# Third layer's linear attention: head products among the next tile's level products, row products behind the sixth level

## The chip, the cores and the metric

The kernel runs on one core of a Trainium2 chip. The metric is the device time of one execution in microseconds (us). Several engines work side by side, each through its own list of instructions in order: TensorE (PE: matrix products, with PEld for the load of the stationary operand), VectorE (DVE), ScalarE (ACT), GpSimd (POOL), and SyncE (SP), which here only issues transfers from memory. They meet at semaphores.

## What is computed

The program runs two transformer blocks of two layers each, in 32-bit floats, on 512 latent tokens and 256 context tokens. The third layer (number 2 in the code) has a mixer that joins a Fourier mix and a gated linear attention. The part that matters, cut from the reference:

```python
def step(S, inp):
    qc, kc, vc, ac = inp
    b = jnp.cumsum(ac, axis=2)
    diff = b[:, :, :, None, :] - b[:, :, None, :, :]
    decay = jnp.exp(jnp.where(mask, diff, -jnp.inf))
    attn = jnp.einsum('bhid,bhjd,bhijd->bhij', qc, kc, decay)
    o = attn @ vc + jnp.einsum('bhid,bhde->bhie', qc * jnp.exp(b), S)
    ...
o_f, s_f = gla_scan(q, k, v, loga[0], s_f)
o_b, s_b = gla_scan(flip(q), flip(k), flip(v), flip(loga[1]), s_b)
o = o_f + flip(o_b)
o = o * lax.rsqrt(jnp.mean(o * o, axis=-1, keepdims=True) + EPS)
```

There are 4 heads with keys of 64 and values of 128. Besides this, each layer's modulation `silu(c) @ w_mod + b_mod` (1,024 by 6,144 per layer) has to be there before that layer starts; the fourth layer's is worked out during the third layer's attention.

## The kernel before

**Tiles and halves.** The 768 tokens are 6 tiles of 128 (`NT = 6`), and each tile has two halves, `dr = 0` and `dr = 1`: the scan forwards and the scan backwards. The loop counts them as `n = 2 * t + dr`, from 0 to 11. Tiles are counted from 0 here.

**Levels.** A decay between two rows of a tile is split by halving: 8 levels per half, in the order `LEVEL_ORDER = (7, 0, 1, 2, 3, 4, 5, 6)`. Level 7 is the diagonal; levels 0 to 6 are blocks of 64 rows down to 1. "Position i" below is the place in this order, 0 to 7. For each position TensorE multiplies the four heads' prepared queries and keys (line 1581) into one of two PSUM slots (`lv`, two slots in turns), and VectorE copies the wanted entries under a mask into the attention buffer `C_AT` (line 2397 at position 0, line 2399 at the others) and frees the slot. TensorE can be two positions ahead, not more.

**What feeds the levels.** VectorE forms exponents as differences of running sums (`differences`, line 2306), ScalarE takes absolute values and exponentials (`level_decays`, lines 3276 to 3282), GpSimd copies halves of queries and keys (`mixed_halves`, line 3589), VectorE multiplies the two (`coarse_products` line 2321, `next_products` line 2324, `products` line 2315). All this is done for later halves between the masks: in a first half after positions 5 and 6 there are two differences for the half after next, and ScalarE's `level_decays(n + 2, 0)` waits for the second of them. Behind the last mask of a second half come five differences in a row.

**Heads.** When both halves of a tile are masked (`L2_attention_ready`), TensorE multiplies `C_AT` with the values and the decayed queries with the carried state, all four heads in a row (line 1600), into PSUM banks 4 and 5 (`go`, one slot). ScalarE squares and sums each head and takes roots (lines 3311 and 3312), VectorE scales and gates (`heads_scaled` line 2374 and 2380, `heads_gated` line 2384) at positions 5 and 6 of the next tile's second half, and TensorE transposes the result (`turn`, line 1566). `C_AT` is one buffer for both halves of a tile, so VectorE waits with a new tile's masks until the heads before are done (`go.full`).

**Modulation.** Between the halves TensorE also does the fourth layer's modulation, twelve weight tiles of 2 MB: `mod_rows` (64 products, line 913) behind the eighth level of each half; ScalarE copies the row out (line 2924); `mod_columns` transposes it (line 922) behind position 2 of the next half; ScalarE copies that out (line 2930). `mod_rows` waits until ScalarE has taken the columns before, and `mod_columns` until it has taken the rows. The weight tiles come over SP's queue into a ring of two buffers; `mod_rows` frees one.

**TensorE's order around the change**, which is written out by hand: the 16 positions of a tile, `mod_rows` behind each 8, then `turn(t - 1)`, then the four heads of tile t, then the next tile. ScalarE's order in half n: `mod_columns` of n - 1; `level_decays`; the copy of `mod_rows`; and at the end of a second half the squares and roots of that tile's heads, which wait for `go.full`.

**Gates.** `GATE` holds two gates per token kind, spread over the partitions by GpSimd-issued transfers (`spread_gates`, line 3641): index 0 for the mixer's residual, index 1 for the feed-forward's.

Of the kernel before, what the change touches and what calls it, by code (L numbers as in the profile page):

```python
# [9 lines left out]
ACT = mybir.ActivationFunctionType  # L10
# [91 lines left out]
def build(nc, d, layers=(0, 1, 2, 3), debug=None):  # L102
# [3 lines left out]
    with ctxs:  # L106
# [360 lines left out]
        C_AT = GB[:, 1, :].rearrange("p (d h i) -> p d h i", d=2, h=4)  # L467
# [9 lines left out]
        def gla_orders():  # L477
            return ([4, 5, 0, 1, 2, 3], [5, 4, 3, 2, 1, 0])
# [396 lines left out]
        def _(pe):  # L875
# [601 lines left out]
            def mixer2():  # L1477
# [90 lines left out]

                for t in range(NT):
                    for dr in range(2):  # L1570
                        for v_ in LEVEL_ORDER:
# [13 lines left out]
                        if 2 in next_of:  # L1585
                            mod_rows(3, 2 * t + dr, 7)
                    if t:
                        turn(t - 1)
                    if t == 0:
                        pe.wait_ge(S("L2_states_ready"), 1)  # L1590
                    pe.wait_ge(S("L2_attention_ready"), 2 * t + 2)
                    b = 4 + place(go)
                    first = [o[0] for o in gla_orders()]
                    for h in range(GLA_H):
                        rows, a = slice((h % 2) * 64, (h % 2) * 64 + 64), h // 2
                        ops = [(C_AT[:, dr, h % 2 * 2 + a, :], C_V[:, t, h * 128:(h + 1) * 128]) for dr in range(2)]
                        ops += [(C_QB[rows, 2 * dr + a, t * 128:(t + 1) * 128], C_S[rows, dr * 6 + t, a * 128:(a + 1) * 128])
                                for dr in range(2) if t != first[dr]]
                        for j, (x, y) in enumerate(ops):
                            m = mm(bank(b + h % 2, 128, a * 128), x, y, start=j == 0, stop=j == len(ops) - 1)  # L1600
                    m.then_inc(go.full, 1)
# [388 lines left out]
        def _(dve):  # L1990
# [273 lines left out]
            def mixer2():  # L2264
# [122 lines left out]
                for n in range(2 * NT):  # L2387
                    t, dr = n // 2, n % 2
                    if t:
                        dve.wait_ge(go.full, t)  # L2390
                    for i, v_ in enumerate(LEVEL_ORDER):
                        ready(lv)
                        data = PS[:, i % 2 * 1024:i % 2 * 1024 + 1024].rearrange("p (s x) -> p s x", s=2)[:, :, 0:256]
                        at = C_AT[:, dr].rearrange("p (s a) i -> p s (a i)", s=2)
# [11 lines left out]
                        if dr == 0 and v_ in (4, 5) and n + 2 < 2 * NT:  # L2406
                            differences(n + 2, [v_ - 2])
                        if dr == 1 and v_ == 4 and t:
                            heads_scaled(t - 1)
# [291 lines left out]
            def paired_down(L, last_channels):  # L2701
# [32 lines left out]
                def added(q, tile, h):  # L2734

                    if (L, q, tile, h) == (0, 0, 0, 0):
                        dve.wait_ge(S("gates_in"), gates_so_far(0))
# [135 lines left out]
            for L in layers:  # L2873
# [4 lines left out]
                dve.wait_ge(S("gates_in"), gates_so_far(L) if L else 32)  # L2878
# [9 lines left out]
        def _(act):  # L2888
# [322 lines left out]
            def mixer2():  # L3211
# [76 lines left out]

                for n in range(2):
                    for part in range(2):  # L3290
                        level_decays(n, part)
                for n in range(2 * NT):
                    t, dr = n // 2, n % 2
                    if n and 2 in next_of:
                        mod_columns(3, n - 1, 7)
                    if dr == 1 and n + 1 < 2 * NT:
                        level_decays(n + 1, 1)
# [10 lines left out]
                    if dr == 1:  # L3308
                        act.wait_ge(go.full, t + 1)
                        for h in range(GLA_H):  # L3310
                            step(A(C_JUNK, bank(4 + h % 2, 128, h // 2 * 128), ACT.Square, accum_out=ST2[:, 32 + h:33 + h]))
                        step(A(ST2[:, 36:40], ST2[:, 32:36], ACT.Sqrt, scale=1.0 / GLA_DV, bias=EPSC))
                        post("head_rms_ready")
# [195 lines left out]
        def _(pool):  # L3509
# [137 lines left out]
            for n, L in enumerate(layers):  # L3647
# [16 lines left out]
                if L == 2:  # L3664
# [5 lines left out]
                    spread_gates(L)  # L3670
# [37 lines left out]
                else:  # L3708
                    pool.wait_ge(S("m_residual_ready"), tiles_before(L, "m") + 1)
                    bring("conv_vectors_in", CONV_ROWS[:, 0:384].rearrange("j (a p) -> j a p", a=3), d["w_ffn_conv_2"][l].rearrange("a (j p) -> j a p", p=128))  # L3710
                    bring("conv_vectors_in", CONV_ROWS[:, 384:512], rows(d["b_ffn_conv_2"][l]))
                if L >= 2:
                    sums_of_down_tokens(L, range(0, 2))
# [40 lines left out]
```

## Time and profile before

| | |
|---|---|
| median of 3 runs | 4030.51 us (4028.72 to 4032.4) |
| the profiled execution's own time | 4025.92 us |
| its span in the trace | 4024.1 us |
| TensorE busy | 3866.8 us, 96% |
| VectorE busy | 2207.2 us, 55% |
| ScalarE busy | 837.5 us, 21% |
| GpSimd busy | 599.3 us, 15% |
| level stage of the third layer, first level product to first output product | 2472.3 to 2621.6 us, 149.3 us |
| TensorE, VectorE, ScalarE busy in that stage | 123.4, 109.2, 77.8 us |

A busy share is a mean over stages with different limits. The span around the stage is 1.8 us shorter than the execution's time, and the profiled execution is 4.6 us below the median of the timed runs. In the timeline a row's start counts from the start of the span, "xN" is how many instructions are merged into the row, and a bracket at the end says how long the engine stood idle before the row and what released it. Matmuls overlap each other by some 0.1 to 0.2 us, so the distance between starts, and not the length, is what a group of products costs TensorE.

### The profile page before, as it was taken

To read this page: it belongs to the slowest core of one execution; us is meant where nothing else is said; L and a number is where in the kernel's file an instruction comes from. 1 tells how busy PE (TensorE), PEld (TensorE's weight loads), DVE (VectorE), ACT (ScalarE), POOL (GpSimd) and SP (SyncE) were. 2 spreads that over 40 slices of the span, in tenths; PEclk is the share of its full clock that TensorE was granted. 3 is DMA by queue.
4 is the path that set the end of the run, shared out by engine and by line. 5 is a ranking of instruction groups with operands and counts; after the bars stand their busy time and mean duration, and the time that the engine had idled before them with its cause. 6 is when DMAs were issued, how large, how long until landed. Compare 5 with 4: busy or idle time off the path is not lost.

```text
span 4024.1 us, 46147 instructions
## 1 busy us (share of the span) xinstructions
PE 3866.8 (96%) x17618; PEld 2307.7 (57%) x17618; DVE 2207.2 (55%) x3634; ACT 837.5 (21%) x1639; POOL 599.3 (15%) x944
## 2 busy tenths in 40 slices
PE   8999999999999999999999998899999999999998
PEld 5677455544455555458744645645555444758863
DVE  0354533366566556544556015737787765438876
ACT  1266111100122322211101114521100012531000
POOL 1000000133222431400132002200000430000023
PEclk9999999999999999999999998999999999999999
DMA  5355021355412222312344212411112452002234
GB/s 190 108 192 185 21 63 53 115 170 175 156 48 91 87 75 74 126 45 92 126 168 146 73 42 85 168 44 53 63 53 73 168 182 68 16 22 84 94 126 162
DMA packets 209784, 410.59 MB, mean 102 GB/s; under 512 B 5939, under 2 KB 92297, under 8 KB 209441
## 3 DMA queue, kind: packets, MB, share of 16 engines
q1 hardware_dynamic: 203712, 386.94, 28.4%
q0 software_dynamic: 5856, 20.73, 1.7%
q8 instruction: 141, 2.31, 0.2%
q14 instruction: 75, 0.61, 0.0%
HBM read 405.49 MB, written 2.16 MB: 101 GB/s over the span
## 4 chain that ended last, share of the span: by engine, by line
PE 88%; DVE 6%; ACT 3%; DMA 1%; issue 1%; POOL 1%; DVEq 0%; ACTq 0%; POOLq 0%; SPq 0%
PE PS L1210 28%; PE PS L1305 19%; PE PS L1170 5%; PE PS L1143 3%; PE PS L1784 3%; PE PS L1121 3%; PE PS L1798 3%; PE PS L913 2%; PE PS L1785 1%; PE PS L1945 1%; PE PS L1955 1%; PE PS L1429 1%; PE PS L1398 1%; PE PS L1123 1%; PE PS L1632 1%
## 5 line engine op out<-in xcount | busy, mean ns | idle before, releaser
L1210 PE MATMUL PS<-UT,RING 128*128 128x384 f32 (+1 forms) x2432 | 693.8, 433 | 10.8 <-ACT BIG L3011 9.7
L1210 PEld LDWEIGHTS PS<-UT,RING 128*128 128x128 f32 x2432 | 461.0, 190 | 205.5 <-issue 15.5
L1210 PE MATMUL PS<-BIG,RING 128*128 128x384 f32 (+1 forms) x1824 | 528.4, 433 | 0.8 <-DVE BIG L2846 0.5
L1210 PEld LDWEIGHTS PS<-BIG,RING 128*128 128x128 f32 x1824 | 346.0, 190 | 147.1 <-DVEq L2020 1.1
L1305 PE MATMUL PS<-RING,BIG 128*128 128x512 f32 x810 | 377.2, 593 | 2.8 <-POOL RES_TMP L3611 1.4
L3606 POOL TENSOR_TENSOR RES_TMP<-BIG 128x128 f32<-128x128 f32 x68 | 35.7, 525 | 1677.5 <-DVE BIG L2852 581.3
L2695 DVE TENSOR_TENSOR RING<-RING 128x512 f32<-128x512 f32 x135 | 107.0, 793 | 273.6 <-DMA RING<-ff_w_dram 161.5
L1305 PEld LDWEIGHTS PS<-RING,BIG 128*128 128x128 f32 x810 | 151.2, 190 | 183.2 <-issue 177.4
L1305 PE MATMUL PS<-RING,GATE 128*128 128x512 f32 x536 | 244.0, 596 | 6.1 <-DVE RING L2698 6.1
L1305 PE MATMUL PS<-RING,RES_TMP 128*128 128x512 f32 x544 | 245.3, 593 | 0.6 <-DVE RING L2698 0.6
L1305 PEld LDWEIGHTS PS<-RING,GATE 128*128 128x128 f32 x536 | 102.1, 191 | 136.6 <-issue 125.3
L1305 PEld LDWEIGHTS PS<-RING,RES_TMP 128*128 128x128 f32 x544 | 102.9, 190 | 131.9 <-issue 125.7
L3011 ACT ACTIVATE BIG<-PS 128x256 f32<-128x256 f32 (+1 forms) x62 | 26.3, 425 | 570.8 <-PE PS L1210 570.1
L1170 PE MATMUL PS<-RING,UT 128*128 128x512 f32 x320 | 139.2, 593 | 2.0 <-issue 1.2
L2110 DVE TENSOR_TENSOR RES_TMP<-PS,GATE 128x512 f32<-128x512 f32 x40 | 27.7, 692 | 206.5 <-PE PS L1170 137.1
L1784 PE MATMUL PS<-UT,RING 128*128 128x512 f32 x256 | 131.2, 594 | 2.3 <-DVE BIG L2490 1.0
L1121 PE MATMUL PS<-UT,RING 128*128 128x512 f32 x256 | 127.7, 594 | 1.0 <-ACT BIG L3222 1.0
L1798 PE MATMUL PS<-UT,RING 128*128 128x512 f32 x256 | 121.3, 599 | 0.0
L1143 PE MATMUL PS<-RING,UT 128*128 128x512 f32 x256 | 113.6, 606 | 2.5 <-ACT BIG L3340 0.9
L2555 DVE SCALAR_TENSOR_TENSOR BIG<-PS,BIG 128x510 f32<-128x510 f32 (+3 forms) x176 | 110.5, 628 | 6.3
L2696 DVE TENSOR_TENSOR RING<-RING 128x512 f32<-128x512 f32 x135 | 105.0, 778 | 0.0
L1170 PEld LDWEIGHTS PS<-RING,UT 128*128 128x128 f32 x320 | 60.0, 190 | 74.2 <-issue 73.2
(467 smaller groups left out, 5821.1 us busy)
## 6 DMA issues: line engine op xcount, KB each, us to landing
RING<-ff_w_dram SPq DMA_DIRECT2D x112, 1024.0 KB, 5.0
RING<-w_mod_dram SPq DMA_DIRECT2D x48, 2048.0 KB, 8.0
RING<-w_ffn_down_dram SPq DMA_DIRECT2D x55, 1024.0 KB, 5.0
RING<-w_ffn_up_dram SPq DMA_DIRECT2D x44, 1024.0 KB, 5.1
RING<-ssm_w_in_dram SPq DMA_DIRECT2D x8, 2048.0 KB, 7.8
RING<-ssm_w_out_dram SPq DMA_DIRECT2D x4, 2048.0 KB, 8.2
RING<-w_even_in_dram SPq DMA_DIRECT2D x4, 2048.0 KB, 8.3
GATE<-gates_dram POOLq DMA_DIRECT2D x12, 512.0 KB, 9.3
```

What stands on the lines that cost most here:

```text
L913: ins = mm(bank(bank_, 128)[32 * c:32 * c + 32, :], CVW[:, 4 * k + lc:4 * k + lc + 32], w[:, k, c * 128:(c + 1) * 128], start=k == 0, stop ...
L1121: m = mm(PS[:, x:x + LAT], a, UT[:, k, 0:LAT], start=k == 0, stop=k == KD - 1)
L1123: m = mm(PS[:, x + 512:x + 512 + nctx], a, UT[:, k, LAT:LAT + nctx], start=k == 0, stop=k == KD - 1)
L1143: m = mm(bank(first_bank + t, cols[1] - cols[0]), inp[:, kk, t * 128:(t + 1) * 128], w[:, k, cols[0]:cols[1]], start=kk == 0, stop=kk == k ...
L1170: m = mm(bank(t), inp[:, kk, t * 128:(t + 1) * 128], w[:, k, :], start=kk == 0, stop=kk == kn - 1)
L1210: m = mm(bank(bank_, n), a[:, k, :], b[:, k, :], start=k == 0, stop=k == 3)
L1305: return mm(bank(banks[name]), a, b, start=s == 0, stop=last)
L1784: mm(PS[:, x:x + LAT], a, UT[:, k, 0:LAT], start=k == 0, stop=k == KD - 1)
L1798: m = mm(bank(4 + q), wz[:, k, q * 128:(q + 1) * 128], UT[:, k, 0:LAT], start=k == 0, stop=k == KD - 1)
L2555: ins = V.scalar_tensor_tensor(y[:, lo:hi], PS[:, x + lo + o:x + hi + o], w(k), y[:, lo:hi], ALU.mult, ALU.add)
L2695: step.go(V.tensor_tensor(t3, b22, b12, ALU.subtract))
L2696: step(V.tensor_tensor(t1, b12, b11, ALU.subtract))
```

## The change

Six things change, all in the third layer.

1. The attention buffer becomes two, used in turns by tile: the old one and `GATE[:, 1, 0, :]`, which VectorE clears once, in half 0 behind position 5. VectorE's wait on the heads moves back by one tile.
2. The heads of tile t - 1 move into the first half of tile t: one head behind each of positions 1, 2, 3 and 4 (behind `mod_columns` where position 2 has both). The last tile's heads stay behind its levels.
3. `mod_rows` moves from behind position 7 to behind position 5, in every half.
4. `turn(t - 1)` stays behind the tile's levels, and now nothing of line 1600 follows it except in the last tile.
5. ScalarE's squares and roots move from the end of half 2t + 1 to half 2t + 2, behind the copy of `mod_columns`.
6. The second gate is brought after the first residual tile instead of at the start of the layer, and waits are counted accordingly.

```diff
-        C_AT = GB[:, 1, :].rearrange("p (d h i) -> p d h i", d=2, h=4)
+        C_AT = tuple(x.rearrange("p (d h i) -> p d h i", d=2, h=4) for x in (GB[:, 1, :], GATE[:, 1, 0, :]))
...
+                def head(t, h):
+                    if h == 0:
+                        if t == 0:
+                            pe.wait_ge(S("L2_states_ready"), 1)
+                        pe.wait_ge(S("L2_attention_ready"), 2 * t + 2)
+                        go_bank[t] = 4 + place(go)
+                    b = go_bank[t]
+                    rows, a = slice((h % 2) * 64, (h % 2) * 64 + 64), h // 2
+                    ops = [(C_AT[t % 2][:, dr, h % 2 * 2 + a, :], C_V[:, t, h * 128:(h + 1) * 128]) for dr in range(2)]
+                    ops += [(C_QB[rows, 2 * dr + a, t * 128:(t + 1) * 128], C_S[rows, dr * 6 + t, a * 128:(a + 1) * 128])
+                            for dr in range(2) if t != first[dr]]
+                    for j, (x, y) in enumerate(ops):
+                        m = mm(bank(b + h % 2, 128, a * 128), x, y, start=j == 0, stop=j == len(ops) - 1)
+                    if h == GLA_H - 1:
+                        m.then_inc(go.full, 1)
...
-                        for v_ in LEVEL_ORDER:
+                        for i, v_ in enumerate(LEVEL_ORDER):
...
                             if v_ == 1 and 2 in next_of and t + dr:
                                 mod_columns(3, 2 * t + dr - 1, 7, MOD_ROWS[2])
-                        if 2 in next_of:
-                            mod_rows(3, 2 * t + dr, 7)
+                            if t and dr == 0 and 1 <= i <= GLA_H:
+                                head(t - 1, i - 1)
+                            if i == 5 and 2 in next_of:
+                                mod_rows(3, 2 * t + dr, 7)
                     if t:
                         turn(t - 1)
-                    if t == 0:
-                        pe.wait_ge(S("L2_states_ready"), 1)
-                    pe.wait_ge(S("L2_attention_ready"), 2 * t + 2)
...
+                for h in range(GLA_H):
+                    head(NT - 1, h)
...
-                    if t:
-                        dve.wait_ge(go.full, t)
+                    if t >= 2:
+                        dve.wait_ge(go.full, t - 1)
...
-                        at = C_AT[:, dr].rearrange("p (s a) i -> p s (a i)", s=2)
+                        at = C_AT[t % 2][:, dr].rearrange("p (s a) i -> p s (a i)", s=2)
...
+                        if n == 0 and v_ == 4:
+                            step(V.memset(GATE[:, 1, 0, :], 0.0))
...
-                    if (L, q, tile, h) == (0, 0, 0, 0):
-                        dve.wait_ge(S("gates_in"), gates_so_far(0))
+                    if L in (0, 2) and (q, tile, h) == (0, 0, 0):
+                        dve.wait_ge(S("gates_in"), gates_so_far(L))
...
-                dve.wait_ge(S("gates_in"), gates_so_far(L) if L else 32)
+                dve.wait_ge(S("gates_in"), gates_so_far(L) - (32 if L in (0, 2) else 0))
...
+                def head_roots(t):
+                    act.wait_ge(go.full, t + 1)
+                    for h in range(GLA_H):
+                        step(A(C_JUNK, bank(4 + h % 2, 128, h // 2 * 128), ACT.Square, accum_out=ST2[:, 32 + h:33 + h]))
+                    step(A(ST2[:, 36:40], ST2[:, 32:36], ACT.Sqrt, scale=1.0 / GLA_DV, bias=EPSC))
+                    post("head_rms_ready")
...
                     if n and 2 in next_of:
                         mod_columns(3, n - 1, 7)
+                    if dr == 0 and t:
+                        head_roots(t - 1)
                     if dr == 1 and n + 1 < 2 * NT:
                         level_decays(n + 1, 1)
...
-                    if dr == 1:
-                        act.wait_ge(go.full, t + 1)
...
+                head_roots(NT - 1)
...
-                    spread_gates(L)
+                    spread_gates(L, (0,))
...
+                    if L == 2:
+                        spread_gates(L, (1,))
```

## Rows read from the trace of the kernel before

**Rows 1.** Page, part 4: shares of the chain that ended last

```profile
PE 88%; DVE 6%; ACT 3%; DMA 1%; issue 1%; POOL 1%; DVEq 0%; ACTq 0%; POOLq 0%; SPq 0%
```

**Rows 2.** Stretches: span, busy PE, PEld, DVE, ACT, POOL, clock, DMA share, GB/s

```profile
2523.31:2532.76 9.45, 7.52 (x132) 6.03 (x131) 7.65 (x14) 7.65 (x22) 2.43 (x9) 1.00 0.12 37
...
2532.76:2548.67 15.91, 12.50 (x164) 10.24 (x165) 11.77 (x22) 8.01 (x16) 5.82 (x20) 1.00 0.71 244
...
2564.40:2569.90 5.50, 5.42 (x84) 4.51 (x81) 4.82 (x8) 0.28 (x1) 2.38 (x10) 0.61 0.03 9
```

**Rows 3.** Stretch, line 1600 alone, tile 1: span, busy PE, PEld, clock, DMA share, GB/s

```profile
2517.56:2522.68 5.12, 5.12 (x32) 4.15 (x32) 1.00 0.90 303
```

**Rows 4.** Timeline, VectorE ahead of tiles 2, 1, 4, 5: start, us, engine, line, idle

```profile
2518.77 2.53 DVE L2306 TENSOR_TENSOR UT<-BIG 128x256 f32<-128x256 f32 x5
...
2523.31 0.73 DVE L2397 COPY_PREDICATED GB<-UT,PS 128x512 f32<-128x512 uint8 x1 [2.00 <-PE PS L1581]
...
2497.80 0.73 DVE L2397 COPY_PREDICATED GB<-UT,PS 128x512 f32<-128x512 uint8 x1 [2.86 <-PE PS L1581]
...
2575.37 0.73 DVE L2397 COPY_PREDICATED GB<-UT,PS 128x512 f32<-128x512 uint8 x1 [3.35 <-PE PS L1581]
...
2599.83 0.73 DVE L2397 COPY_PREDICATED GB<-UT,PS 128x512 f32<-128x512 uint8 x1 [1.12 <-PE PS L1581]
```

**Rows 5.** Timeline, first half of tile 2, TensorE and VectorE

```profile
2524.09 0.71 PE L1581 MATMUL PS<-UT 64*128 64x128 f32 x8 [0.45 <-DVE GB L2397]
...
2524.74 0.33 PE L922 MATMUL PS<-CS,RES_TMP 128*128 128x128 f32 x1
...
2524.92 0.45 DVE L2399 COPY_PREDICATED GB<-UT,PS 128x256 f32<-128x256 uint8 x1 [0.40 <-PE PS L1581]
...
2524.99 1.16 PE L1581 MATMUL PS<-UT 64*128 64x128 f32 x16
...
2529.25 0.73 DVE L2399 COPY_PREDICATED GB<-UT,PS 128x256 f32<-128x256 uint8 x1
...
2529.44 1.95 PE L913 MATMUL PS<-RING,CVW 128*32 128x128 f32 x64
...
2531.32 0.71 PE L1581 MATMUL PS<-BIG 64*128 64x128 f32 x8
```

**Rows 6.** Timeline, tile 2, ScalarE and what follows from it

```profile
2525.79 0.28 ACT L3311 ACTIVATE UT<-PS 128x128 f32<-128x128 f32 x1
...
2527.38 1.28 ACT L3312 ACT_TABLE_LOAD   x1
...
2528.67 0.30 ACT L3312 ACTIVATE ST<-ST 128x4 f32<-128x4 f32 x1
...
2530.55 1.65 ACT L3276 ACTIVATE UT<-BIG 128x128 f32<-128x128 f32 x6 [1.29 <-DVEq L2020]
...
2536.57 0.44 DVE L2399 COPY_PREDICATED GB<-UT,PS 128x256 f32<-128x256 uint8 x1 [0.99 <-PE PS L1581]
```

**Rows 7.** Timeline, second half of tile 2

```profile
2537.15 0.72 PE L1581 MATMUL PS<-UT 64*128 64x128 f32 x8 [0.19 <-DVE GB L2399]
...
2540.47 0.75 DVE L2399 COPY_PREDICATED GB<-UT,PS 128x256 f32<-128x256 uint8 x1
```

**Rows 8.** Line 2296, the other clearing of a 1,024-column buffer: ns min/median/max

```profile
L2296 DVE MEMSET GB<- x1: 912/912/912, 2439.6 to 2439.6; 128x1024 f32 x1
```

**Rows 9.** Timeline, first half of the last tile and the step behind it

```profile
2604.85 2.03 DVE L2399 COPY_PREDICATED GB<-UT,PS 128x256 f32<-128x256 uint8 x3
...
2609.44 0.73 DVE L2397 COPY_PREDICATED GB<-UT,PS 128x512 f32<-128x512 uint8 x1 [1.39 <-PE PS L1581]
```

**Rows 10.** Timeline, row product in tile 3 at the low clock

```profile
2566.07 3.23 PE L913 MATMUL PS<-RING,CVW 128*32 128x128 f32 x64
```

**Rows 11.** Buffer GATE from 2440 to 3300 us: first product with the second gate

```profile
L2741 DVE TENSOR_TENSOR GATE<-GATE x6: 691/826/828, 3185.0 to 3264.2; 128x512 f32<-128x512 f32 x6
```

**Rows 12.** Page, part 6: KB each, us to landing

```profile
RING<-w_mod_dram SPq DMA_DIRECT2D x48, 2048.0 KB, 8.0
```

More of the change, by code:

```diff
@@ L1567, in turn @@
                     m.then_inc(gt.full, 1)
+                first = [o[0] for o in gla_orders()]
+                go_bank = {}
+                def head(t, h):
[13 more added lines that the diff above has]
+                        m.then_inc(go.full, 1)
                 for t in range(NT):
                     for dr in range(2):
-                        for v_ in LEVEL_ORDER:
+                        for i, v_ in enumerate(LEVEL_ORDER):
                             if v_ in (0, 4):
@@ L1584, in mixer2 @@
                                 mod_columns(3, 2 * t + dr - 1, 7, MOD_ROWS[2])
-                        if 2 in next_of:
-                            mod_rows(3, 2 * t + dr, 7)
+                            if t and dr == 0 and 1 <= i <= GLA_H:
+                                head(t - 1, i - 1)
+                            if i == 5 and 2 in next_of:
+                                mod_rows(3, 2 * t + dr, 7)
                     if t:
                         turn(t - 1)
-                    if t == 0:
-                        pe.wait_ge(S("L2_states_ready"), 1)
-                    pe.wait_ge(S("L2_attention_ready"), 2 * t + 2)
[L1592 to L1601, printed above, removed]
+                for h in range(GLA_H):
+                    head(NT - 1, h)
                 if 2 in next_of:
@@ L3307, in mixer2 @@
                         level_decays(n + 2, 1)
-                    if dr == 1:
-                        act.wait_ge(go.full, t + 1)
[L3310 to L3313, printed above, removed]
+                head_roots(NT - 1)
                 if 2 in next_of:
```

## The prediction

> **What bounds the kernel now.** I read the page's chain of waits first [rows 1]: TensorE holds most of it, but that is the mean of a long program, and the change touches one stage of 149 us. So I went to the busy time by stretch of one ordinary tile there, tile 2 [rows 2]. Its first half takes 9.45 us and its second 15.91. In the first half TensorE and VectorE are busy 7.52 and 7.65 us, in the second 12.50 and 11.77: two engines that hand work to each other, neither full. What counts is who waits where, and that is in the timeline.
>
> Between two tiles VectorE waits. Its five differences end at 2518.77 + 2.53 = 2521.30, and its first mask of tile 2 starts only at 2523.31, after 2.00 us of idling on TensorE [rows 4]. TensorE was then behind with the row product and the four heads, 5.12 us for 32 instructions, which is 1.28 us a head [rows 3]. The same wait is 2.86 us ahead of tile 1, 3.35 ahead of tile 4 and 1.12 ahead of tile 5 [rows 4]; ahead of tile 3 it is as in tile 2. Inside the first half it is VectorE that paces: TensorE's 64 products of line 913 run from 2529.44 to 2531.32, and VectorE needs what follows them only at the end of the half [rows 2, 5]. In that half the row product costs nothing today.
>
> **The change, part by part.**
>
> **The wait between tiles goes.** With the heads moved, TensorE has only the transposes and positions 0 and 1 to do there (0.65 us a position [rows 5], from 2524.09 to 2524.74), while VectorE is busy 2.53 us with the differences alone. The second attention buffer lets the first mask start. So the mask comes when the differences end: 2.00 us earlier in each of tiles 2 and 3. Ahead of tile 4 I also take 2.00 and not 3.35, since the 1.35 between them stands behind a row product that took 3.23 us instead of 1.95 at a low clock [rows 5, 10], which the change doesn't remove. Ahead of tile 5 it is 1.12. Late next is VectorE itself.
>
> **The heads and the row product lengthen the first half.** TensorE works in order, so everything put among the positions pushes the later ones. The first head is free: it is issued during the differences, before VectorE begins the tile. From there I add up TensorE's path in tile 2 from the start of position 2 at 2524.09, which waits for the first mask as now [rows 5]: position 2, 0.65; columns, 0.25 (2524.74 to 2524.99); three heads, 3 x 1.28 = 3.84; positions 3, 4 and 5, 3 x 0.65 = 1.95; row product, 1.88 (2529.44 to 2531.32). That is 8.57 us, so position 6 starts at 2532.66. A mask starts 0.83 us after its products (2524.09 to 2524.92), so that of position 6 starts at 2533.49. Today it starts at 2529.25. **The delay is 4.24 us.** VectorE can't make it up: in this stretch it has only masks and products that each wait for the position before.
>
> The delay passes on whole. The second difference behind that mask is what ScalarE waits for at 2530.55, after idling 1.29 us [rows 6]; the exponentials that follow release the row's copy, the columns, position 3 of the second half and, at 2536.57 after 0.99 us of idling, VectorE. That chain moves by the same 4.24, and so does VectorE's own.
>
> **The squares and roots** move with the heads. ScalarE is waiting for the last head with the level decays and the copy of the rows queued behind it, and TensorE's columns wait for that copy. The last head ends 0.65 + 0.25 + 3.84 + 2 x 0.65 = 6.04 us after 2524.09, at 2530.13. The squares take 1.59 (2525.79 to 2527.38), the table load and the root 1.59 more (to 2528.67 + 0.30) [rows 6], so they end at 2533.31. The exponents come 1.30 us behind the mask of position 6 (2529.25 to 2530.55), at 2534.79. The cover is 1.5 us and this costs nothing; without it each microsecond would go straight into the second half.
>
> **The row product of a second half** is hidden there. Position 5 starts at 2537.15 [rows 7]; with 0.65 + 1.88 + 0.83 the mask of position 6 can start at 2540.51, against 2540.47 now, because VectorE scales the heads in between. Cost 0.04, taken as nothing. Then the transposes: they still wait for the gating, and positions 0 and 1 behind them have the time of the differences.
>
> **Tile 0** has no heads in its first half. It gets the clearing of the second buffer, and the nearest row is the same instruction on another buffer of 1,024 columns, 0.91 us [rows 8]. Its second half has no scaling to hide the row product, which costs between 0 and 1.88 us. Against these stands the wait of 2.86. The sum lies between -1.95 and -0.07; I take the middle, -1.0.
>
> **The last tile.** The heads that move into its first half are those of tile 4, where one direction starts and a head has 6 instructions instead of 8: an estimate of 0.96 us each from [rows 3]. The path becomes 7.61 us, and the mask of position 6 starts 0.78 + 7.61 + 0.83 = 9.22 us after the first mask. Today it is the second of the three masks that begin at 2604.85 [rows 9], some 0.48 later, which is 5.50 us after the first at 2599.83. Delay 3.72; less 1.39, the wait ahead of the second half [rows 9], which stood for a row product that comes earlier now. Its second half has a thinner VectorE and nothing for the half after next, so the row product costs 0 to 1.88 us; I take 0.95. Together +3.3. The last heads stay where they were.
>
> **Costed at nothing**: the second gate is fetched behind the first residual tile, and its first use is at 3185.0 [rows 11], over 500 us later; GpSimd has only the two issues more there and two fewer at the layer's start. SP's queue: the row products free its weight buffers a few us earlier or later, a load takes 8.0 us [rows 12], and a buffer is wanted again a tile later, some 25 us [rows 2]; if that cover went, one load would show. VectorE's new wait on the heads of two tiles ago is long past.
>
> **Sum**: tile 0 -1.0; tiles 1, 2 and 3, 3 x (4.24 - 2.00) = +6.7; tile 4, 4.24 - 1.12 = +3.1; tile 5 +3.3. Together +12.1 us. Against the profiled execution's own 4025.92 us that is 4038.0; the median of the runs shown lies 4.6 us above that execution, so the forecast on its scale is 4042.6 us, 0.30% slower. A measurement of this kernel can tell about 0.2%, 8 us, from no change.
>
> **The rivals.**
>
> **Faster.** The heads fall into TensorE's gaps and only the waits between tiles change: 2.86 + 2 x 2.00 + 3.35 + 1.12 = 11.3 us, which gives 4019. For it: TensorE idles 1.93 + 3.41 us in a tile [rows 2], more than the heads that VectorE waits for. Against it: the point at which it decides is the room in the first half, 1.93 us, and three heads with the row product bring 5.72. It needs the heads to overlap the positions, and in the rows nothing on TensorE does.
>
> **Within 0.2%.** The row product of a first half stays hidden, as in the second: 5 x 1.88 = 9.4 us fewer, 4033. It decides by VectorE's work behind position 5, one mask and one difference, 0.9 us, against 1.88. Against it is also that each of these masks waits for TensorE in the sum, so VectorE has nothing in store.
>
> **The clock.** TensorE's granted clock was 0.61 of full speed on average from 2564.40 to 2569.90 [rows 2], a time partly at 1.2 instead of 2.4 GHz, and a row product took 3.23 us there instead of 1.95 [rows 5, 10], 1.66 times as long. Ahead of it TensorE had the thin start of a second half; the same start in tile 2 went by at 1.00 [rows 2]. The change makes first halves dense, and the starts of second halves no denser. A first half that falls into the low clock lengthens by up to 0.66 x 8.57 = 5.7 us; two of them give 4054. Now these products are on VectorE's path, so a fall costs more than today. The Trainium skill, TensorE: Matmul & The Clock Gate, section "HAM oscillation", says that gaps between groups of matmuls drop the clock again and that work without gaps keeps it up. By that rule the first halves would hold the clock and the risk would lie with the second halves; no run here shows that yet.
>
> **How the numbers follow.** The forecast has 0.62, with a range of its own of 4037 to 4049 us: the two halved bounds give 1.9 us, the clock of one half 5.7. The clock rival has 0.13, within 0.2% 0.13, faster 0.12. The range from 4030 to 4056 takes in the small rival and most of the clock's; left out are the faster case and a tail, 0.17. Slower by over 0.2% lies above 4038.6: 0.55 of the forecast's share and the clock's 0.13, 0.68. Same: 0.20. Faster: 0.12.
>
> **What would show it.** In the changed profile VectorE's 2 us wait ahead of each tile is gone; in first halves of tiles 1 to 4 the mask of position 6 starts 10.2 us after the first mask instead of 5.9; new waits of VectorE on line 1581 stand ahead of the masks of positions 3, 4, 5 and 6; a tile takes 27.6 us instead of 25.4. It is wrong if a first half stays near 9.5 us, if ScalarE ends the roots after the exponents, or if the row product of a second half shows.

## The result and the profile after

The changed kernel takes 4068.72 us (4067.85 to 4073.6) against 4029.61 for the kernel before on the same chip: 1.0096 times as long, 95% interval 1.0084 to 1.0108. The sign is as forecast, the size three times as large: 39 us, not 12, and outside the range.

Head and part 1 of the page of the changed kernel:

```profile
span 4066.8 us, 46148 instructions
...
PE 3894.7 (96%) x17618; PEld 2332.0 (57%) x17618; DVE 2206.4 (54%) x3635; ACT 837.4 (21%) x1639; POOL 596.8 (15%) x944
```

VectorE, ScalarE and GpSimd are as busy as before; TensorE runs the same 17,618 products and is busy 28 us longer. So it is the same work, done slower or waited for.

A half runs from VectorE's first mask of that half to its first mask of the next (line 2397, now 2407). In us, with the granted clock as a share of full speed:

| | first half, tiles 1 / 2 / 3 / 4 / 5 | second half, tiles 0 / 1 / 2 / 3 / 4 |
|---|---|---|
| before | 9.45 / 9.45 / 9.46 / 9.45 / 9.61 | 14.31 / 16.06 / 15.91 / 17.24 / 15.01 |
| after | 17.39 / 17.48 / 15.88 / 17.42 / 16.28 | 13.20 / 16.53 / 16.54 / 15.71 / 16.20 |
| clock before | 1.00 / 1.00 / 1.00 / 1.00 / 1.00 | 1.00 / 0.89 / 1.00 / 0.80 / 1.00 |
| clock after | 0.71 / 0.71 / 0.79 / 0.71 / 0.69 | 0.87 / 0.79 / 0.79 / 0.78 / 0.79 |

First halves are 37.0 us longer in sum, second halves 0.4 shorter; tile 0's first half adds 0.9 (10.74 for 9.84) and the last tile's second half with its heads 3.8 (15.97 for 12.17, up to the first output product). That is the whole 41.4 us of the stage; some 2 us more stand behind it, in output products that still run at the low clock. The rows of tile 2, to set beside [rows 2] (stretch, busy PE, PEld, DVE, ACT, POOL, clock, DMA share, GB/s):

```profile
2530.51:2547.99 17.48, 15.07 (x153) 12.79 (x153) 7.57 (x14) 9.27 (x25) 2.05 (x9) 0.71 0.18 52
...
2547.99:2564.53 16.54, 11.43 (x141) 9.52 (x141) 11.73 (x23) 6.38 (x14) 5.79 (x20) 0.79 0.57 202
```

VectorE works as long as before in either half. The timeline of the same tile:

```profile
2527.36 0.71 PE L1584 MATMUL PS<-BIG,GATE 128*128 128x128 f32 x4
...
2527.77 2.52 DVE L2316 TENSOR_TENSOR UT<-BIG 128x256 f32<-128x256 f32 x5
...
2530.51 0.73 DVE L2407 COPY_PREDICATED GB<-UT,PS 128x512 f32<-128x512 uint8 x1 [0.22 <-DVE UT L2316]
...
2531.29 0.71 PE L1600 MATMUL PS<-UT 64*128 64x128 f32 x8 [2.58 <-DVE GB L2407]
...
2537.61 1.22 PE L1584 MATMUL PS<-BIG,GATE 128*128 128x128 f32 x4
...
2540.76 3.08 PE L913 MATMUL PS<-RING,CVW 128*32 128x128 f32 x64
...
2542.89 0.30 ACT L3305 ACTIVATE ST<-ST 128x4 f32<-128x4 f32 x1
...
2544.53 0.72 DVE L2409 COPY_PREDICATED GB<-UT,PS 128x256 f32<-128x256 uint8 x1 [2.77 <-PE PS L1600]
...
2545.80 1.65 ACT L3288 ACTIVATE UT<-BIG 128x128 f32<-128x128 f32 x6 [2.62 <-DVEq L2030]
```

The wait ahead of the tile is gone, as forecast: the mask at 2530.51 follows the differences and no longer TensorE [rows 4]. In its place TensorE has idled 2.58 us when it starts position 2 at 2531.29. Soon after that everything it does takes longer: four instructions of a head 1.22 us, where those of the first head took 0.71 at 2527.36, and the row product 3.08 instead of 1.95 [rows 5]. The mask of position 6 starts at 2544.53, which is 14.0 us after the first mask; the forecast had 10.2, and it was 5.9 before. The clock in finer stretches of that tile:

```profile
2528.60:2531.29 2.69, 0.10 (x1) 0.00 (x1) 2.29 (x6) 2.38 (x8) 1.41 (x4) 1.00 0.82 308
...
2531.29:2532.80 1.51, 1.51 (x15) 1.27 (x17) 0.88 (x2) 1.39 (x2) 0.00 (x0) 1.00 0.00 0
...
2533.00:2543.00 10.00, 10.00 (x88) 8.71 (x88) 3.11 (x6) 4.60 (x13) 1.94 (x8) 0.50 0.01 2
...
2543.70:2545.30 1.60, 1.23 (x24) 0.97 (x16) 0.74 (x2) 0.00 (x0) 0.00 (x0) 1.00 0.21 22
...
2545.30:2550.79 5.49, 2.15 (x24) 1.60 (x25) 4.80 (x9) 4.78 (x10) 1.69 (x6) 0.92 0.99 350
...
2550.79:2555.00 4.21, 4.21 (x41) 3.66 (x45) 2.29 (x6) 1.86 (x3) 0.06 (x1) 0.50 0.12 41
```

TensorE idles (0.10 us of work in 2.69), goes on at full speed for some 1.6 us, and then stands at the lower of its two levels, 1.2 GHz, for some ten us, though it never stops working in them. Then full speed again; a thin start of the second half (2.15 us of work in 5.49); then the lower level once more. The first halves of tiles 1, 4 and 5 look like this too; in tile 3 the clock came back earlier (15.88 us at 0.79).

### The profile page after: what moved, and what is told of

It reads as the page before. It is cut to its first block, busy times and chain, and to the rows that moved or that the text cites. A ratio compares the mean times of both kernels' runs of the same rounds, so it can differ in the third digit from the quotient of the medians.

```text
span 4066.8 us, 46148 instructions
## 1 busy us (share of the span) xinstructions
PE 3894.7 (96%) x17618; PEld 2332.0 (57%) x17618; DVE 2206.4 (54%) x3635; ACT 837.4 (21%) x1639; POOL 596.8 (15%) x944
## 4 chain that ended last, share of the span: by engine, by line
PE 89%; DVE 5%; ACT 3%; issue 1%; DMA 1%; POOL 0%; DVEq 0%; ACTq 0%; SPq 0%; POOLq 0%
PE PS L1210 27%; PE PS L1305 19%; PE PS L1170 5%; PE PS L1143 3%; PE PS L1794 3%; PE PS L1121 3%; PE PS L1808 3%; PE PS L913 2%; PE PS L1795 1%; PE PS L1955 1%; PE PS L1965 1%; PE PS L1429 1%; PE PS L1398 1%; PE PS L1600 1%; PE PS L1123 1%
## 5 line engine op out<-in xcount | busy, mean ns | idle before, releaser
L913 PE MATMUL PS<-RING,CVW 128*32 128x128 f32 x3072 | 104.0, 293 | 0.4 <-DMA RING<-w_mod_dram 0.4
```

The lines of the kernel that those rows point to most:

```text
L913: ins = mm(bank(bank_, 128)[32 * c:32 * c + 32, :], CVW[:, 4 * k + lc:4 * k + lc + 32], w[:, k, c * 128:(c + 1) * 128], start=k == 0, stop ...
```

## The experiments

Theory A: the forecast's count is right at full speed, and what it lacked is the clock, which falls because the change leaves TensorE idle ahead of position 2 (and thinly used at the start of a second half). Rivals: B, the mix of head and level products is slow by itself; C, the row product in the middle of the half does the harm and the clock is secondary. For each run the table has the ratio to the kernel before with its interval, and means over tiles 1 to 4.

| run | median us | ratio | first half, clock | second half, clock |
|---|---|---|---|---|
| before | 4029 to 4030 | | 9.45, 1.00 | 16.06, 0.92 |
| after | 4068.72 | 1.0096 (1.0084 to 1.0108) | 17.04, 0.73 | 16.25, 0.79 |
| e1 | 4046.19 | 1.0041 (1.0027 to 1.0055) | 12.75, 1.00 | 16.28, 0.79 |
| e2 | 4040.57 | 1.0027 (1.0016 to 1.0037) | 12.55, 0.89 | 15.31, 0.83 |
| e3 | 4058.80 | 1.0070 (1.0053 to 1.0087) | 13.17, 0.91 | 16.90, 0.90 |
| e4 | 4028.04 | 0.9997 (0.9987 to 1.0006) | 9.45, 1.00 | 16.12, 0.90 |
| e5 | 4025.09 | 0.9985 (0.9976 to 0.9994) | 10.66, 1.00 | 14.74, 0.80 |
| e6 | 4039.65 | 1.0024 (1.0015 to 1.0033) | 12.75, 1.00 | 14.21, 1.00 |
| e7 | 4043.82 | 1.0034 (1.0021 to 1.0048) | 9.84, 1.00 | 17.52, 0.81 |
| e8 | 4021.16 | 0.9978 (0.9969 to 0.9987) | 11.76, 0.84 | 13.39, 0.93 |
| e9 | 4025.91 | 0.9989 (0.9980 to 0.9999) | 9.67, 1.00 | 14.81, 0.97 |
| e10 | 4057.88 | 1.0079 (1.0063 to 1.0095) | 16.11, 0.78 | 14.19, 1.00 |
| e11 | 4023.36 | 0.9985 (0.9976 to 0.9994) | 9.66, 0.98 | 13.96, 0.98 |

### e1: the idle place ahead of position 2 filled

```diff
                                 head(t - 1, i - 1)
+                                if i == 1:
+                                    for _ in range(7):
+                                        mm(bank(4, 128, 256), ident, ident, start=True, stop=True)
```

> The changed kernel with seven extra 128x128 products behind each first head (tiles 1 to 5), into a corner of PSUM that nothing reads; 14 instructions at 0.16 us, about 2.2 us, in the place where TensorE idles 2.6 us between its first head and position 2. Theory A (that idling lets TensorE's clock fall, and the fall is what the forecast lacked): first halves of tiles 1 to 3 go from 17.4 to about 13.7 us at a granted clock near 1.0 instead of 0.71, the program takes 4037 to 4049 us. Theory B (the low clock comes from the thin second halves or from the mix of head and level products itself): first halves stay at 17 us and 0.7, the program stays at 4065 to 4072 us.

Stretches of tile 2, and TensorE's timeline in it:

```profile
2527.65:2540.42 12.77, 10.37 (x153) 8.78 (x153) 7.59 (x13) 9.27 (x24) 2.25 (x9) 1.00 0.24 72
...
2540.42:2556.13 15.71, 12.84 (x155) 10.89 (x155) 11.86 (x22) 6.39 (x14) 5.83 (x20) 0.78 0.58 210
```

```profile
2528.43 0.72 PE L1600 MATMUL PS<-UT 64*128 64x128 f32 x8 [0.84 <-DVE GB L2410]
...
2529.78 0.37 PE L1584 MATMUL PS<-BIG 64*128 64x128 f32 x1
...
2529.80 0.37 PE L1600 MATMUL PS<-UT 64*128 64x128 f32 x1
...
2534.32 1.96 PE L913 MATMUL PS<-RING,CVW 128*32 128x128 f32 x64
...
2541.20 1.22 PE L1600 MATMUL PS<-UT 64*128 64x128 f32 x8 [1.32 <-DVE GB L2410]
...
2546.66 2.32 PE L913 MATMUL PS<-RING,CVW 128*32 128x128 f32 x64
```

Adding work made the program 23 us faster than the changed kernel. First halves run at full speed in all five tiles and take 12.77 us instead of 17.48 in tile 2. B is out: the mix of products is not slow by itself. It is even cheaper than counted. Rows of line 1584 (heads) and line 1600 (levels) stand 0.02 us apart at 2529.78 and 2529.80: products of 64 rows from either overlap. From position 2 to the row product it is 2534.32 - 2528.43 = 5.89 us, where the forecast's terms make 6.69. The second halves are as slow as in the changed kernel: position 2 starts at 2541.20 after 1.32 us of idling and takes 1.22 us, and the row product 2.32.

### e10 and e6: the other two corners

The same with three such products behind position 1 of a second half and three behind position 2, in the slots of `lv` that TensorE holds then; e10 has these alone, e6 has them and those of e1.

```diff
-                            b = place(lv) * 2
+                            if not (t and dr and i == 3):
+                                b = place(lv) * 2
...
+                            if t and dr and i == 1:
+                                for _ in range(3):
+                                    m = mm(bank(b, 128, 256), ident, ident, start=True, stop=True)
                             m.then_inc(lv.full, 1)
+                            if t and dr and i == 2:
+                                b = place(lv) * 2
+                                for _ in range(3):
+                                    mm(bank(b, 128, 256), ident, ident, start=True, stop=True)
```

> The changed kernel with the idle products in the second halves alone, the idling ahead of position 2 left open. With e1 (first place filled alone) and e6 (both) this makes the four corners. If each place sets the clock of what follows it: first halves stay near 17.4 us at 0.71, second halves go to about 14.2, the program to 4052 to 4060 us. If the second place also feeds the next first half, first halves drop too and the program comes under 4048 us.

> The kernel of e1 with six more idle products in each second half of tiles 1 to 5: three behind position 1, three ahead of the columns behind position 2, where TensorE idles 1.3 us twice; nothing reads them. Theory A2 (the second halves run long because the clock falls behind that thin start, and the row product behind position 5 then stands on VectorE's path): clock near 1.0 in both halves, second halves 14.0 us instead of 15.7 to 16.9, first halves 12.8 as in e1, the program at 4032 to 4038 us. If the second halves' length has another cause: clock near 1.0 but 15.7 to 16.9 us, the program at 4043 to 4050 us.

Stretches of e10: first and second half of tile 1, first half of tile 2; then TensorE's position 2 in the first half of tile 3:

```profile
2495.82:2513.17 17.35, 15.48 (x157) 13.26 (x158) 7.56 (x13) 8.70 (x23) 1.98 (x9) 0.70 0.22 70
...
2513.17:2527.41 14.24, 10.19 (x151) 8.22 (x149) 11.85 (x22) 6.45 (x15) 5.89 (x20) 1.00 0.66 238
...
2527.41:2541.72 14.31, 12.44 (x158) 10.72 (x159) 7.58 (x13) 9.28 (x24) 2.25 (x9) 0.88 0.20 64
...
2556.68 1.23 PE L1601 MATMUL PS<-UT 64*128 64x128 f32 x8 [2.58 <-DVE GATE L2415]
```

Stretches of e6, first and second half of tile 2:

```profile
2522.27:2535.04 12.77, 10.90 (x158) 9.38 (x159) 7.58 (x13) 9.27 (x24) 2.24 (x9) 1.00 0.24 74
...
2535.04:2549.23 14.19, 11.88 (x164) 9.79 (x163) 11.78 (x22) 6.40 (x14) 5.83 (x20) 1.00 0.66 236
```

The corners come apart cleanly. Where a place is filled the half behind it runs at 0.99 to 1.00, in every tile from 1 to 5 for the first place and from 1 to 4 for the second; where it isn't, it doesn't, whatever the other place does. In e10 the open place gave 17.35 us in tile 1 but 14.31 in tile 2: the same idling, of 2.6 us, is paid for with different lengths of low clock. In tile 3 the clock was low before TensorE went back to work: position 2 itself took 1.23 us. e6 is the forecast's own kernel at full speed: halves of 12.8 and 14.2 us, where the forecast's terms give 13.7 and 13.9. Its median is 10 us above before, 1.7 above what was expected. That makes the 39 us, as an estimate, some 10 of order and some 29 of clock; what the idle products themselves cost is not told apart. (The executions of e6 spread from 4033.4 to 4044.0 us, those of the kernel before beside them from 4025.4 to 4036.1.)

### e2: only the heads moved

The changed kernel with `if i == 7` instead of `if i == 5` ahead of `mod_rows`.

> The changed kernel with the modulation's row product back behind position 7 in every half. Theory A: the idling ahead of position 2 is still there, so the first halves still run at about 0.7, shorter only by the row product of about 3 us at the low clock: 14 us each, the program at 4048 to 4060 us. Theory C (the row product in the middle of a first half is what makes it long; the clock is secondary): first halves near 11.8 us at a clock near 1.0, the program at 4030 to 4036 us.

TensorE's rows at position 2 of tiles 1, 2, 4 and 5, and the first halves of tiles 1, 2 and 4:

```profile
2501.50 0.71 PE L1600 MATMUL PS<-UT 64*128 64x128 f32 x8 [1.40 <-DVE GATE L2407]
...
2528.18 1.01 PE L1600 MATMUL PS<-UT 64*128 64x128 f32 x8 [1.88 <-DVE GB L2407]
...
2582.40 0.71 PE L1600 MATMUL PS<-UT 64*128 64x128 f32 x8 [2.55 <-DVE GB L2407]
...
2612.96 0.71 PE L1600 MATMUL PS<-UT 64*128 64x128 f32 x8 [2.77 <-DVE GATE L2407]
```

```profile
2500.72:2511.75 11.03, 10.10 (x153) 8.67 (x153) 7.53 (x13) 7.91 (x22) 2.16 (x9) 1.00 0.42 161
...
2527.39:2540.06 12.67, 11.65 (x153) 10.01 (x153) 7.55 (x13) 8.54 (x23) 2.24 (x9) 0.87 0.28 105
...
2581.61:2597.01 15.40, 14.53 (x153) 12.78 (x153) 7.50 (x13) 8.91 (x24) 2.04 (x9) 0.67 0.18 70
```

Neither expectation fits. The row product behind position 7 now uses up part of the idle place, differently in each tile, and that makes the run worth having: after 1.40 us of idling the half runs at 1.00 and takes 11.03 us, after 1.88 at 0.87 and 12.67, after 2.55 at 0.67 and 15.40. In these tiles, and in tile 3 (0.37 us of idling, 11.11 us at 1.00), the first half's length goes with the idling ahead of it. Tile 5 does not fit: it had the longest idling, 2.77 us, and ran at 0.85, for 11.50 us. C is out: in tile 4 the row product isn't there, and the half is still slow; in e1 it is there, and the half takes 12.77 us at full speed.

### e3 and e7: only the row product moved

In the kernel before, with the heads where they were:

```diff
-                        if 2 in next_of:
-                            mod_rows(3, 2 * t + dr, 7)
+                            if i == 5 and 2 in next_of:
+                                mod_rows(3, 2 * t + dr, 7)
```

> The kernel before with only the row product moved behind position 5 in every half; the heads stay behind each tile. By the forecast's way of counting the second halves of tiles 1 to 3 lose 1.9 us each of VectorE's wait and the first halves gain 0.5 (position 5 is early there without heads), tile 4 loses 0.6, tile 0 about 1: the program 4 to 7 us faster than before, 4023 to 4026 us, at a clock near 1.0 throughout. If the row product in a first half is as costly as in the changed kernel, the program is level with the kernel before or slower, 4029 to 4036 us.

TensorE's row product in the first half of tile 2:

```profile
2539.45 3.28 PE L913 MATMUL PS<-RING,CVW 128*32 128x128 f32 x64 [2.20 <-ACT MODC L2930]
```

This was not the test that was meant. `mod_rows` waits for ScalarE's copy of the columns before, and in the old order that copy stands behind the squares and roots: 2.20 us of waiting. The program is slower than either expectation. The clock goes with this wait too, though no head stands among the positions: in tile 1 TensorE waited 1.54 us and the first half stayed at 1.00, in tiles 2 to 5 it waited 2.19 to 3.07 us and they ran at 0.88. e7 puts ScalarE in the changed kernel's order as well:

```diff
...
                         mod_columns(3, n - 1, 7)
+                    if dr == 0 and t:
+                        head_roots(t - 1)
...
-                    if dr == 1:
-                        act.wait_ge(go.full, t + 1)
...
+                head_roots(NT - 1)
```

> The kernel of e3 (row product behind position 5, heads where they were) with ScalarE's squares and roots behind the copy of the columns, as in the changed kernel. In e3 TensorE waited 2.2 to 3.1 us ahead of each first half's row product for that copy. Without this wait the first halves come to 10 us instead of 13.7, the second to 16 to 17 if the low clock stays, the program to 4035 to 4043 us; 4029 to 4033 us if the clock holds. If that wait was not the cause, it stays at 4055 us or more.

Halves of tile 2, and in its second half VectorE's mask of position 6 and the transposes:

```profile
2530.60:2540.44 9.84, 7.53 (x133) 6.06 (x131) 7.70 (x13) 7.64 (x21) 2.24 (x9) 1.00 0.28 85
...
2540.44:2558.21 17.77, 14.74 (x164) 12.38 (x165) 11.84 (x22) 8.03 (x16) 5.82 (x20) 0.81 0.55 193
```

```profile
2550.03 0.72 DVE L2399 COPY_PREDICATED GB<-UT,PS 128x256 f32<-128x256 uint8 x1 [1.23 <-PE PS L1581]
...
2551.59 0.66 PE L1566 MATMUL PS<-CS,GB 128*128 128x128 f32 x4 [1.23 <-DVEq L2020]
```

First halves go to 9.84 us: in them the row product costs 0.4, close to the forecast's count for a half without heads (0.5 in e3's text). The second halves are 1.5 us longer than before, and the program 14 us. Before, the row product stood behind position 7, where TensorE waits for the gating anyway, and filled it. Now that place is 1.23 us of idling, and the row product stands ahead of position 6, in a half at 0.81 of the clock, so VectorE waits 1.23 us for that position. Why the clock is lower in these halves than before, 0.81 for 0.92, no run shows. The forecast had this move at nothing.

### e8: idling without the change

The kernel before with `ops = ops[:1]` for each head: one product is done, the others are left out.

> The kernel before with one of the four products of each head (of the three in tiles 4 and 5) done and the others left out: the backward half of the attention and the carried state are missing from the heads. TensorE is short of 3.8 us of work between tiles and idles there instead, and VectorE's wait of 2.0 us ahead of a tile goes. If idling there by itself drops the clock (theory A without the head products among the levels), first halves run at 0.7 to 0.9 and take 10 to 11 us instead of 9.45. If the fall needs the products that follow, the clock stays at 1.0 in first halves, they take 9.4 us, and the program is 7 to 11 us faster than before, 4018 to 4022 us.

TensorE in the first halves of tiles 2, 3 and 5, and the stretch of tile 5's:

```profile
2519.21 0.72 PE L1581 MATMUL PS<-UT 64*128 64x128 f32 x8 [1.33 <-DVE GB L2398]
...
2526.22 3.64 PE L913 MATMUL PS<-RING,CVW 128*32 128x128 f32 x64 [1.58 <-ACT MODC L2931]
...
2545.21 0.81 PE L1581 MATMUL PS<-UT 64*128 64x128 f32 x8 [2.49 <-DVE GB L2398]
...
2594.87 0.72 PE L1581 MATMUL PS<-UT 64*128 64x128 f32 x8 [2.48 <-DVE GB L2398]
...
2594.09:2604.61 10.52, 6.93 (x127) 5.75 (x129) 6.71 (x11) 7.39 (x18) 0.00 (x0) 1.00 0.27 102
```

Inconclusive on the clock. The idle place came out at 1.33 us in tile 2 and 1.34 in tile 4, at 2.49 in tile 3 and 2.48 in tile 5, and in tiles 2, 4 and 5 a wait of 1.6 us for ScalarE's copy follows, which the earlier heads had delayed. Tile 3 fell behind the idle place and again later (12.15 us at 0.72), so the clock can fall without head products behind it. Tile 2 fell in the second wait (0.77). Tiles 4 and 5 had the same two waits as tile 2, or longer ones, and stayed at 1.00. So idling of 2.5 us makes a fall possible and does not settle it. The program gained 9 us, as was expected with the wait between tiles gone and first halves at 9.4 us; but first halves came to 11.76 and second halves to 13.39, so that agreement shows nothing.

### e4, e5 and e9: the heads in the idle place

Heads 0, 1 and 2 behind position 1, head 3 behind position 4; the row product behind position 7 in first halves. In second halves it stands behind position 5 in e4 and behind 7 in e5. e9 is e5 with the idle products of e6's second halves.

```diff
-                            if t and dr == 0 and 1 <= i <= GLA_H:
-                                head(t - 1, i - 1)
-                            if i == 5 and 2 in next_of:
+                            if t and dr == 0 and i in (1, 4):
+                                for h in ((0, 1, 2) if i == 1 else (3,)):
+                                    head(t - 1, h)
+                            if i == (7, 5)[dr] and 2 in next_of:
```

> The changed kernel with the heads 0, 1 and 2 behind position 1 (where TensorE idles) and head 3 behind position 4, the row product behind position 7 in first halves and behind position 5 in second halves. Theory A: no idling of over 1.5 us is left between tiles, the clock stays near 1.0; first halves near 10 us, second halves near 13.9, the program 5 to 10 us faster than before, 4019 to 4025 us. Theory B: the clock falls to 0.7 to 0.8 as in the changed kernel and the program takes 4045 us or more.

> The kernel of e4 (heads 0, 1, 2 behind position 1, head 3 behind position 4) with the row product behind position 7 in second halves too, as in the kernel before. In e4 the second halves took 15.6 to 16.4 us because a row product at the low clock (3.4 us) stood ahead of position 6. If that is what e4 loses, its second halves come to about 14.0 to 14.5 us here even where the clock falls, and the program to 4015 to 4022 us. If the heads behind position 1 cost the second halves something else (a later exponent chain), they stay at 15.5 to 16.4 and the program at 4026 to 4031 us.

> The kernel of e5 with six idle products in each second half of tiles 1 to 5, at the places of e6; nothing reads them. If the low clock of e5's second halves (0.76) is what is left of their length, the clock goes to about 1.0, second halves from 14.4 to 15.1 down to about 14.0 us, first halves from 10 to 11.4 down to 9.5 (in e5 the late row product pushed the heads), and the program to 4015 to 4020 us. If the first halves are long for their own reasons, they stay at 10 to 11 and the program at 4022 to 4026 us.

e4 in the second half of tile 2:

```profile
2538.64 3.42 PE L913 MATMUL PS<-RING,CVW 128*32 128x128 f32 x64
...
2542.83 0.72 DVE L2410 COPY_PREDICATED GB<-UT,PS 128x256 f32<-128x256 uint8 x1 [1.67 <-PE PS L1600]
```

With three heads in the idle place first halves are back at 9.45 us and 1.00, so four heads cost nothing there. The program is still 3 us above what was expected. What e4 loses is in second halves: the row product at the low clock, 3.42 us, stands ahead of position 6, and VectorE waits 1.67. e5 puts it back and takes second halves to 14.74 us, but at the low clock the late row product pushes the heads, and first halves come to 10.66. It is 0.15% faster than before, a miss by 3 us of what was expected. e9 has first halves back at 9.67, and shows that the clock is not all of it: at 0.97 second halves stay at 14.8, and the program at 4025.91 us, 6 above what was expected if the clock were all.

### e11: real work in the second idle place

The kernel of e5 with the first half's row product behind position 1 of the second half, and its columns behind position 3.

```diff
-                            if v_ == 1 and 2 in next_of and t + dr:
+                            if i == (2, 3)[dr] and 2 in next_of and t + dr:
...
-                            if i == 7 and 2 in next_of:
-                                mod_rows(3, 2 * t + dr, 7)
+                            if dr and i in (1, 7) and 2 in next_of:
+                                mod_rows(3, 2 * t + i // 7, 7)
```

> Real work instead of idle products: the kernel of e5 with the first half's row product moved to behind position 1 of the second half (where TensorE idles 1.3 us twice), and its columns behind position 3 instead of 2, so that position 3 no longer waits for ScalarE's chain. By the count of rows: first halves 9.5 us, second halves 13 to 13.5 us (0.9 less than with the wait), the clock near 1.0, the program 4010 to 4018 us. If the clock falls all the same: second halves over 14 us and 4020 us or more.

Halves of tile 2, and in it the row product, the columns, and VectorE's mask of position 4:

```profile
2526.98:2536.44 9.46, 7.70 (x103) 6.29 (x105) 7.67 (x13) 8.64 (x23) 2.43 (x9) 1.00 0.30 113
...
2536.44:2550.13 13.69, 11.92 (x205) 9.88 (x193) 11.90 (x23) 7.04 (x16) 5.86 (x20) 1.00 0.70 233
```

```profile
2535.84 1.95 PE L913 MATMUL PS<-RING,CVW 128*32 128x128 f32 x64
...
2539.90 0.33 PE L922 MATMUL PS<-CS,RES_TMP 128*128 128x128 f32 x1 [1.02 <-ACT RES_TMP L2937]
...
2541.00 0.43 DVE L2410 COPY_PREDICATED GB<-UT,PS 128x256 f32<-128x256 uint8 x1 [0.30 <-PE PS L1600]
```

Halves of 9.46 and 13.69 us with the clock at 1.00: a tile takes 23.15 us for 25.36 before. Tile 3's second half still fell, to 0.93 and 14.97. The program is 0.15% faster than before, 4023.36 us, 5 us short of what was expected; the profiled executions place the stage's gain at 7.5 us from first mask to the last tile's second half, but the stage began some 4 us later in e11's profile than in that of the kernel before, and what follows it took some 4 us longer; why is not shown. It beats the changed kernel by 45 us; the 0.15% by which it beats the kernel before is less than the 0.2% that the prediction takes as what a measurement can tell.

## Why the prediction was wrong

**The wait between tiles.** Right. VectorE's first mask follows the differences in every tile, and that part of the gain is real: second halves of 14.2 us in e6, against 13.9 forecast.

**The first half.** The path was right, the durations were not. Its terms came from rows at full speed [rows 5], and the step that failed is the assumption that they would hold behind the new order: the first half of tile 2 grew by 8.03 us (17.48 for 9.45), where the sum has 4.24. At full speed the sum was even too long: e6 has 12.77 us where the terms give 13.69, because products of heads and levels overlap. The prediction says that nothing on TensorE does; the trace of the kernel before shows it, outside the prediction's rows, where the last head (line 1600) meets the next position (line 1581) 0.01 us apart:

```profile
2547.41 0.37 PE L1600 MATMUL PS<-BIG 64*128 64x128 f32 x1
...
2547.42 0.37 PE L1581 MATMUL PS<-BIG 64*128 64x128 f32 x1
```

What the sum lacked is the clock: with it held, in e6, the program is some 10 us slower than before, near the forecast's 12.

**The clock rival.** It named the mechanism and its price per half (5.7 us at most; measured 17.48 - 12.77 = 4.7 in tile 2), gave it two halves and a chance of 0.13, and put the risk at the wrong place. The forecast itself says what is left for TensorE between tiles, the transposes and two positions, while VectorE is busy with its differences. What these leave of VectorE's time, less the first head, is TensorE's idle time; both were in the text, it was never worked out, and the changed kernel has it at 2.58 us. The longest idling between products of TensorE from the first mask to the last in the kernel before is 1.28 us (one of 2.40 ends just ahead, at 2472.30, with the clock already at 0.50), so the trace of before did not show what such a gap does at full speed, and that called for a wide upper bound. The sentence from the Trainium skill (TensorE: Matmul & The Clock Gate, "HAM oscillation") was weighed the wrong way round: that gaps between groups of matmuls drop the clock is what the trace shows, and the gap was the one that the change makes. The dense half behind it did not hold the clock up: in tile 2 it ran some ten us at the low level before the clock came back.

**The row product of a second half.** Forecast at 0.04 us; e7, with the heads left alone, has second halves 1.5 us longer each in tiles 1 to 4 and the program some 14 us slower, most of it in second halves. Two things were missing: behind position 7 it had filled a wait of TensorE, and behind position 5 it is on VectorE's path as soon as the clock is low, since 0.65 + 1.88 + 0.83 fits the cover [rows 7] only at full speed. That e2 (11 us) and e7 (14) make less than the change (39) points to an interaction, the moved row product no longer filling what the moved heads leave open; e2's shorter idling in tiles 1 to 3 fits it.

**Squares and roots.** Right in kind: they end at 2543.19 and the exponents come at 2545.80, so nothing waits for them, though both are later than forecast.

**Gates and the second buffer.** In e6, where the clock is not in the way, the stage accounts for all of the difference; the fetch of the second gate shows nowhere. Tile 0's first half is 0.8 us longer there (10.64), as the 0.91 of [rows 8] has it. No run had these parts alone.

**What stays open**: what settles whether the clock falls behind such idling (tile 5 of e8 had 2.48 us and stayed at 1.00), and how long it then stays low. e10 had 17.35, 14.31, 18.45, 14.32 us in four tiles with 2.6 us of idling ahead of each.

## What to carry to other kernels

When work is moved out of an engine's wait, work out what that engine then does in the place it leaves. On TensorE an idle place is not free even where nobody waits for it: here it mostly cost several us of halved speed in the work behind, which had just become the critical one. A tight order should put the moved products into the idle place first (e4's first halves) and only the rest between steps, and a price read from rows at full speed needs a second price at the lower level wherever the order ahead of it changes.

## What was not expected of the hardware

Adding products that nobody reads made the program 23 us faster (e1) and 29 us faster (e6) than the changed kernel. After idling of 1.40, 1.88 and 2.55 us the first half ran at a granted clock of 1.00, 0.87 and 0.67 (e2), but after 2.77 us at 0.85 (e2) and after 2.48 us at 1.00 (e8). And in tile 2 of the changed kernel the clock fell some 1.6 us after TensorE had gone back to work, not in the idling itself, and came back only some ten us later, with TensorE at work all the time; in tile 3 of e10 it had fallen before the idling was over.
